# Reordering the FFN's first product pair, its passage from up to down, and its last squares in a fused two-layer block

## The chip, the cores and the metric

One core of one Trainium2 chip runs the whole program once per launch. The metric is device microseconds of that core, the median of several runs. The engines work side by side, each with its own in-order instruction stream, and meet at semaphores: PE (TensorE), ACT (ScalarE), DVE (VectorE), POOL (GpSimd) and SP (SyncE, which here only issues DMAs). ACT can issue DMAs too, on a queue of its own.

## The reference

A sequence of 1024 tokens with 1024 features goes through two layers. The change lies in the feed-forward part (FFN) of the first layer and in what stands next to it:

```python
    u2 = _rmsnorm(h, ln2_g[i])
    a, bb = jnp.split(u2 @ w_gate_upffn[i], 2, axis=-1)      # 1024 -> 2 x 2816
    h = h + (jax.nn.silu(a) * bb) @ w_down[i]                # 2816 -> 1024
    u3 = _rmsnorm(h, ln3_g[i])
    gate = jax.nn.sigmoid(u3 @ w_ple_gate[i])
    h = h + gate * (p[i] @ w_ple_proj[i])                    # p: 256 -> 1024
```

Before it stand gated linear attention and a convolution with their projection; after it a second layer with window attention.

## The kernel before

All tensors are held feature-major, 128 partitions by 1024 tokens per tile. Each fp32 operand is split in a rounded high part (`_hi`) and a rest (`_lo`), and each product is three matmuls (hi·hi, hi·lo, lo·hi). The FFN's matrix products are done by a seven-product scheme (Strassen and Winograd's), so for each weight slot `w` there are seven combinations `r = 0..6` of quarters of the weights and of the operand.

**The projection of p** (`gemm4`, L751) is the last thing ahead of the FFN: eight output tiles of 1024 tokens, written to the PSUM halves G[0] and G[1] in turn, and copied out by ACT (`projected_p`, L1417) to `pj_out`, from where SP sends them to memory.

**The up stage** has 22 slots, w = 0..21 (`UP` = 22), even ones for `a` in G, odd ones for `bb` in U. `product(w, r)` (L939) does 12 matmuls of 512 columns: it waits for `ring_lo` of (w, r), for w < 2 also for `X_lo[r]`, and for the PSUM banks to be read. The first and the last two slots (0 and 1; 20 and 21) go in the order of the list `FIRST`: (0,0) (0,1) (1,0) (1,1) (0,2) (0,3) (1,2) (1,3) (0,4) (0,5) (0,6) (1,4) (1,5) (1,6). ACT rounds weights (`weights_hi`, L1425 to L1433, to `ring_hi`) and operands (`operand_hi`, L1435, to `X_hi`); DVE makes the rests (`weights_lo` L2090, `operand_lo` L2083), the normalised input (`normed_x` L2066, four instructions each) and the operand's differences (`turn_x` L2072). POOL makes the weights' sums S (`sums_of`, L606). ACT and DVE read the products from PSUM (`take` L1448, `quarter` L2095), and ACT's `silu` (L1462) and DVE's `gated_quarter` (L2110) end a pair of slots, which is a group.

**The hidden values.** A group's result `cb` is turned into seven pieces by four DVE differences (`turn_h`, L2118). Each piece is rounded by ACT (`hidden_hi`, L1467), its rest is made by DVE (`hidden_lo`, L2129), both in `hst[q % 2]`, two buffers used in turn, and SP sends it to `hid_spill` in memory (`hidden_out`, L468). With 11 groups there are 77 pieces, q = 0..76; the last group's are 70 to 76. ACT may write a buffer only when the DMA of two pieces before has landed (semaphores `hs_out`).

**The down stage** reads the pieces back, two groups (a chunk) at a time, as 14 DMAs of 512 KB (`chunk_in`, L476) into Dc[0] (0 to 56 KB of each partition, where X_hi[0..3] and X_lo[0..3] lie) or Dc[1] (56 to 112 KB). `down_product` (L967) does 12 matmuls a slot and r, in two halves m; products 4, 5 and 6 wait until DVE has added the first products of the same slot to `h` (`down_add`, L2184 to L2196). `h` itself was sent to memory before the FFN and comes back in two DMAs of 2 MB (`h_in`), since `cb` and `hst` lie in its place. Each engine's order is written out by hand. SP's order in the passage from up to down: weights of slot 22, pieces 63 and 64, chunk 0 rows 0 to 3, pieces 65 and 66, chunk 0 rows 4 to 6, pieces 67 to 69, weights 23, first half of h, pieces 70 and 71, and so on (`chunks_in`, L500 to L531).

**The end of the FFN.** In the last slot (`LAST` = 32) DVE puts four squares (`add_square`) among its adds; POOL makes the rests of A3's tiles 0 to 3 and then both parts of the first weight slot of the next product (`split(1, S_PLE)`, L642). Behind that PE starts `gemm(1, S_PLE, ...)`, and then `gemm(0, S_PLE + 1, ...)`, ahead of whose tile 1 it sums the squares (`quarter_sums`) and ahead of whose tile 4 it spreads the inverse root (`spread`, L925 to L931).

## Time and profile before

| | us |
|---|---|
| median of three runs | 1735.76 (1732.69 to 1735.9) |
| the profiled execution, by itself | 1733.72 |
| its span, first to last instruction | 1731.9 |
| PE busy | 1648.4 (95%) |
| DVE / POOL / ACT busy | 1167.1 / 703.1 / 623.9 |
| mean granted TensorE clock | 0.986 of full |

Spans are read from the first instruction's start; us from the span's start are called times below. PE's own share of 95% leaves some 83 us in which it is idle, and the mean clock of 0.986 tells of stretches in which it ran at half speed.

### The profile page before, as it was taken

The page shows a single profiled execution, that of the slowest core. Times are in us where ns is not written, and L with a number is a line of the kernel's source. Part 1 is how long each engine was busy: PE and PEld are TensorE (multiplying, and loading weights), DVE is VectorE, ACT ScalarE, POOL GpSimd, SP SyncE. Part 2 cuts the span into 40 slices and gives each one's busy share as a digit, 9 for nine tenths or more (in the row PEclk, how much of TensorE's full clock was granted, in tenths as well). Part 3 has the DMA queues.
Part 4 walks back from the last instruction along what each step waited for, and adds up shares of the span by engine and source line. Part 5 has one row for each costly group of instructions (what it writes and reads, how often), then busy time and mean ns, then how long its engine had stood idle before and what let it go on. Part 6 is the DMA issues. An engine that isn't in the chain of part 4 may idle for free.

```text
span 1731.9 us, 21560 instructions
## 1 busy us (share of the span) xinstructions
PE 1648.4 (95%) x7810; PEld 1358.0 (78%) x7810; DVE 1167.1 (67%) x1697; ACT 623.9 (36%) x976; POOL 703.1 (41%) x381
## 2 busy tenths in 40 slices
PE   9999999999979999999997899999879999999996
PEld 6888787878868888888885788877658888889775
DVE  7232898953497777776757566878856983685457
ACT  5131333321345444444433122254451111277214
POOL 2534111144423332332226587652255554452451
PEclk9999999999999999999999999999999999999998
DMA  5411110141613434334377966041101111100012
GB/s 189 82 49 39 35 37 25 37 158 49 219 61 134 158 135 164 151 147 169 151 285 283 374 267 269 27 158 49 37 12 49 48 49 49 61 26 1 25 37 97
DMA packets 52421, 190.24 MB, mean 110 GB/s; under 512 B 5681, under 2 KB 7618, under 8 KB 51562
## 3 DMA queue, kind: packets, MB, share of 16 engines
q1 hardware_dynamic: 49378, 178.95, 28.5%
q10 hardware_dynamic: 2952, 10.10, 2.3%
q8 instruction: 55, 0.90, 0.2%
q14 instruction: 36, 0.29, 0.1%
HBM read 133.97 MB, written 55.05 MB: 109 GB/s over the span
## 4 chain that ended last, share of the span: by engine, by line
PE 56%; DVE 8%; DMA 3%; issue 3%; ACT 2%; POOL 1%; POOLq 0%; DVEq 0%; ACTq 0%
PE G L730 15%; PE U L962 11%; PE G L962 10%; PE U L1000 5%; PE G L1000 5%; PE G L1036 2%; PE U L1210 2%; DMA hid_spill<-hst 2%; PE G L1197 1%; PE G L1116 1%; PE U L1079 1%; DVE h L2196 1%; DVE B_lo L1821 1%; DMA h<-h_spill 0%; DVE hst L2132 0%
## 5 line engine op out<-in xcount | busy, mean ns | idle before, releaser
L581 POOL TENSOR_SCALAR w_hi<-raw 128x1024 fp32r<-128x1024 f32 x51 | 152.8, 2997 | 298.4 <-PE G L730 220.6
L730 PE MATMUL G<-B_hi,w_hi 128*128 128x512 f32 x512 | 161.3, 396 | 5.1 <-DVE h L2054 2.8
L730 PE MATMUL G<-B_lo,w_hi 128*128 128x512 f32 x512 | 158.7, 391 | 0.0
L730 PE MATMUL G<-B_hi,w_lo 128*128 128x512 f32 x512 | 158.5, 391 | 0.0
L730 PE MATMUL G<-A_hi,w_hi 128*128 128x512 f32 x448 | 144.6, 404 | 2.9 <-DVE h L2196 2.8
L730 PE MATMUL G<-A_lo,w_hi 128*128 128x512 f32 x448 | 138.9, 391 | 0.0
L730 PE MATMUL G<-A_hi,w_lo 128*128 128x512 f32 x448 | 138.6, 391 | 0.0
L583 POOL TENSOR_TENSOR w_lo<-raw,w_hi 128x1024 fp32r<-128x1024 f32 x51 | 134.6, 2639 | 4.3
L619 POOL TENSOR_TENSOR S<-fraw 128x512 f32<-128x512 f32 x33 | 45.9, 1390 | 217.4 <-DVE ring_lo L2093 200.1
L962 PE MATMUL U<-X_hi,ring_hi 128*128 128x512 f32 x308 | 121.4, 394 | 9.6 <-DVE ring_lo L2093 9.6
L1433 ACT ACTIVATE ring_hi<-S 128x512 fp32r<-128x512 f32 x132 | 82.1, 628 | 115.2 <-PE U L1000 76.4
L962 PE MATMUL G<-X_hi,ring_hi 128*128 128x512 f32 x308 | 120.1, 390 | 2.5 <-ACT pj_out L1420 1.2
L962 PE MATMUL U<-X_lo,ring_hi 128*128 128x512 f32 x308 | 120.8, 392 | 0.0
L962 PE MATMUL U<-X_hi,ring_lo 128*128 128x512 f32 x308 | 120.8, 392 | 0.0
L962 PE MATMUL G<-X_lo,ring_hi 128*128 128x512 f32 x308 | 119.9, 389 | 0.0
L962 PE MATMUL G<-X_hi,ring_lo 128*128 128x512 f32 x308 | 119.8, 389 | 0.0
L730 PEld LDWEIGHTS G<-B_hi,w_hi 128*128 128x128 f32 x512 | 96.3, 190 | 27.5 <-DVE h L2054 3.2
L730 PEld LDWEIGHTS G<-B_lo,w_hi 128*128 128x128 f32 x512 | 96.9, 189 | 20.5
L730 PEld LDWEIGHTS G<-B_hi,w_lo 128*128 128x128 f32 x512 | 96.7, 189 | 20.3
L1433 ACT ACTIVATE ring_hi<-fraw 128x512 fp32r<-128x512 f32 x99 | 61.8, 627 | 114.6 <-PE U L1000 61.0
L1000 PE MATMUL G<-Dc,ring_hi 128*128 128x512 f32 x280 | 88.5, 398 | 14.3 <-DVE h L2196 14.3
L730 PEld LDWEIGHTS G<-A_hi,w_lo 128*128 128x128 f32 x448 | 84.4, 188 | 18.2
(377 smaller groups left out, 3837.2 us busy)
## 6 DMA issues: line engine op xcount, KB each, us to landing
hid_spill<-hst SPq DMA_DIRECT2D x77, 512.0 KB, 2.6
raw<-in_weights SPq DMA_DIRECT2D x72, 512.0 KB, 3.6
Dc<-hid_spill SPq DMA_DIRECT2D x70, 512.0 KB, 7.8
fraw<-in_weights SPq DMA_DIRECT2D x66, 512.0 KB, 4.5
h<-in_x_t SPq DMA_DIRECT2D x8, 512.0 KB, 7.7
h<-in_x_t ACTq DMA_DIRECT2D x1, 4096.0 KB, 15.1
h_spill<-h SPq DMA_DIRECT2D x8, 512.0 KB, 6.7
pj_spill<-pj_out SPq DMA_DIRECT2D x8, 512.0 KB, 2.6
```

What stands on the lines that cost most here:

```text
L581: pool.tensor_scalar(hi, raw[:, u, :], 1.0, None, ALU.mult).then_inc(w_hi_done, 1)
L583: pool.tensor_tensor(lo, raw[:, u, :], f(hi), ALU.subtract).then_inc(w_split, 1)
L619: pool.tensor_tensor(s1, a21, a22, ALU.add).then_inc(s_sum, 1)
L730: mm = pe.matmul(G[g][:, b * HT:(b + 1) * HT], w, x[:, k, b * HT:(b + 1) * HT], start=s0, stop=s1)
L962: mm = pe.matmul(banks[x][BANK_OF[r]], a, b[r][:, k, :], start=(r < 4 and k == 0 and n == 0), stop=(k == 3 and n == 2), skip_group_check=( ...
L1000: mm = pe.matmul(banks[m][BANK_OF[r]], a, b, start=(r < 4 and n == pairs[0] and e == 0), stop=(n == pairs[-1] and e == 2), skip_group_chec ...
L1036: mm = pe.matmul(G[g][:, hs(n)], a, x[:, kk, hs(n)], start=(kk == 0 and e == 0), stop=(kk == KT - 1 and e == 2))
L1079: mm = pe.matmul(U[:, b, g * P:(g + 1) * P], first, sm[:, n, row, :], start=True, stop=True)
L1116: mm = pe.matmul(G[u][:, hs(n)], w, x[:, k, hs(n)], start=(k == 0 and not low and e == 0), stop=(k == KT - 1 and low == 1))
L1197: mm = pe.transpose(G[0][:, hd % 2 * HT + kb * P:hd % 2 * HT + (kb + 1) * P], scores_of(n, par, hd)[:, kb * P:(kb + 1) * P], ident[:, :])
L1210: mm = pe.matmul(U[:, 2 + par, c0:c0 + HD], pT[:, hd % 2, kb, :], vv, start=(kb == 0), stop=(kb == nkb - 1))
L1433: act.activation(ring(ring_hi, w, r), combo(w, r), ACT.Copy).then_inc(f_hi[w % 2], 1)
```

## The change

It has three parts. In the first pair, the last tile of the projection of p is computed and copied out by halves of 512 tokens (new semaphore `p_half`, new function `last_projected`), and ACT's and DVE's orders are changed. In the passage, the last five pieces get buffers of their own (`hst_last`, seven with the two of `hst`), the 14 DMAs of chunk 0 move from SP's queue to ACT's (`first_chunk_in`), SP's order is changed, and ACT rounds the last seven pieces in one run. At the end, the high part of weight slot S_PLE moves from POOL to ACT, and two of the four squares move behind the adds.

```diff
+        hst_last = [at(f"hst_last{j}", kb, [P, 2, HT], F32R) for j, kb in enumerate((96, 100, 104, 108, 196))]
...
+        def piece_of_pair(q):
+            own = q - NR * (GROUPS - 1) - 2
+            return hst[:, q % 2, :, :] if own < 0 else hst_last[own][:, :, :]
...
             def hidden_out(q):
+                landed_in = hs_out[q % 2] if q < NR * (GROUPS - 1) + 2 else hs_last
                 sp.wait_ge(hl_done, q + 1)
...
             last = NR * (GROUPS - 2)
-            hidden_out(last), hidden_out(last + 1)
-            chunks_in(0, UP - 1, 0, 1, 2, 3)
-            hidden_out(last + 2), hidden_out(last + 3)
-            chunks_in(0, UP - 1, 4, 5, 6)
-            for j in range(4, NR):
+            for j in range(NR):
                 hidden_out(last + j)
             raw_in(UP + 1)
...
             h_in(0)
             last += NR
-            hidden_out(last), hidden_out(last + 1)
+            for j in range(NR):
+                hidden_out(last + j)
+            for u in range(2):
+                sp.wait_ge(hs_out[u], 16 * (last // 2 + 1))
+            h_in(1)
             raw_in(UP + 2)
-            hidden_out(last + 2), hidden_out(last + 3)
-            for j in range(4, NR):
-                chunks_in(1, UP - 1, j - 4)
-                hidden_out(last + j)
-            landed(GROUPS)
-            h_in(1)
-            chunks_in(1, UP - 1, 3, 4, 5, 6)
+            chunks_in(1, UP - 1, 0, 1, 2, 3, 4)
+            sp.wait_ge(hs_last, 16 * len(hst_last))
+            chunks_in(1, UP - 1, 5, 6)
             raw_in(UP + 3)
...
-            pool.wait_ge(f_used[0], used(LAST, 2))
-            split(1, S_PLE, bufs[1], wait=False)
+            weights_low(S_PLE, bufs[1])
...
                 if w == 0 and r == 0:
+                    pe.wait_ge(p_half, 2)
+                if w == 0 and r == 1:
                     pe.wait_ge(acc_free[0], (C_PLE + 1) // 2)
...
+                elif r == 3:
+                    act.wait_ge(w_split, S_PROJ + 2)
...
+                if q >= NR * (GROUPS - 1) + 2:
+                    act.wait_ge(f_used[1], used(UP - 1, NR - 1))
+                elif q >= 2:
...
+            def last_projected():
+                g = (C_PROJ + KT - 1) % 2
+                act.wait_ge(p_half, 1)
+                act.activation(pj_out[:, (KT - 1) % 2, (KT - 1) // 2, 0:HT], G[g][:, 0:HT], ACT.Copy).then_inc(p_half, 1)
+                act.wait_ge(acc_done, C_PROJ + KT)
+                act.activation(pj_out[:, (KT - 1) % 2, (KT - 1) // 2, HT:T], G[g][:, HT:T], ACT.Copy).then_inc(acc_free[g], 1)
...
+            def first_chunk_in(r):
+                for n in range(2):
+                    act.dma_start(f(Dc[0][:, r, n, :, :].rearrange("p a n -> p (a n)")), hid_spill[n, :, r, :]).then_inc(ch_in[0][r], 16)
...
                     hidden_hi(NR * (GROUPS - 2) + hi_at[k])
+                if x and r < 4:
+                    first_chunk_in(2 * r)
+                    if r < 3:
+                        first_chunk_in(2 * r + 1)
             last = NR * (GROUPS - 1)
-            hidden_hi(last), hidden_hi(last + 1)
+            for j in range(NR):
+                hidden_hi(last + j)
             for w in range(UP, LAST):
                 for r in range(NR):
                     weights_hi(w + 1, r)
-                    if w == UP and r < 5:
-                        hidden_hi(last + 2 + r)
...
+            act.wait_ge(f_used[0], used(LAST, 2))
+            slot_hi(S_PLE, w_hi[:, 1, :], wait=False)
             act.wait_ge(f_used[0], used(LAST, 5))
...
             turn_h(last, 0), hidden_lo(NR * last), turn_h(last, 1), hidden_lo(NR * last + 1), turn_h(last, 2)
+            hidden_lo(NR * last + 2), hidden_lo(NR * last + 3), turn_h(last, 3)
             dve.wait_ge(h_back[0], 16)
             for r in range(NR):
                 down_add(r, 0, UP, 0, 0)
-                if r < 5:
-                    hidden_lo(NR * last + 2 + r)
-                if r == 2:
-                    turn_h(last, 3)
+                if r < 3:
+                    hidden_lo(NR * last + 4 + r)
...
-                    if w == LAST and r < 4:
+                    if w == LAST and r < 2:
                         add_square(r % 2, 2 * KT + r, 2 * KT + r)
```

`gemm4` gets the argument `halves`, with which its last tile does the six matmuls of tokens 0 to 511 and then the six of tokens 512 to 1023. The two squares taken out stand among the four `A_lo` instructions behind the adds.

The first pair on DVE, from the eight instructions of the normalised input on (`X_lo_101` to `_104` are X_lo[0] to X_lo[3], `ring_lo_126`, `_127`, `_128` are r = 0, 1, 2, `fraw_110` is slot 0's weights and `fraw_111` slot 1's). Before:

```order
L2070 SCALAR_TENSOR_TENSOR h<-h,vecs,U 128x512 x8
L2088 TENSOR_TENSOR X_lo_101<-h,X_hi_94 128x2048
L2093 TENSOR_TENSOR ring_lo_126<-fraw_110,ring_hi_119 128x512
L2093 TENSOR_TENSOR ring_lo_127<-fraw_110,ring_hi_120 128x512
L2088 TENSOR_TENSOR X_lo_102<-h,X_hi_95 128x2048
L2070 SCALAR_TENSOR_TENSOR h<-h,vecs,U 128x512 x4
L2081 TENSOR_TENSOR T1x<-h 128x2048
L2093 TENSOR_TENSOR ring_lo_128<-S_133,ring_hi_121 128x512
L2070 SCALAR_TENSOR_TENSOR h<-h,vecs,U 128x512 x4
L2093 TENSOR_TENSOR ring_lo_126<-fraw_111,ring_hi_119 128x512
```

Now (`ring_lo_131`, `_132`, `_133` are the same three buffers):

```order
L2106 SCALAR_TENSOR_TENSOR h<-h,vecs,U 128x512 x8
L2124 TENSOR_TENSOR X_lo_101<-h,X_hi_94 128x2048
L2124 TENSOR_TENSOR X_lo_102<-h,X_hi_95 128x2048
L2129 TENSOR_TENSOR ring_lo_131<-fraw_110,ring_hi_124 128x512
L2129 TENSOR_TENSOR ring_lo_132<-fraw_110,ring_hi_125 128x512
L2106 SCALAR_TENSOR_TENSOR h<-h,vecs,U 128x512 x4
L2117 TENSOR_TENSOR T1x<-h 128x2048
L2129 TENSOR_TENSOR ring_lo_133<-S_138,ring_hi_126 128x512
L2129 TENSOR_TENSOR ring_lo_131<-fraw_111,ring_hi_124 128x512
L2106 SCALAR_TENSOR_TENSOR h<-h,vecs,U 128x512 x4
```

X_lo[1] has moved ahead of the first two weight rests, and slot 1's first rest ahead of the last four instructions of the normalised input. On ACT, `X_hi[0]` and `X_hi[1]` have moved ahead of the first three `ring_hi`.

The passage on DVE, from the first difference of the last group on. Before:

```order
L2127 TENSOR_TENSOR T1h<-cb 128x512
L2132 TENSOR_TENSOR hst<-cb,hst 128x512
L2127 TENSOR_TENSOR cb<-cb 128x512
L2132 TENSOR_TENSOR hst<-cb,hst 128x512
L2127 TENSOR_TENSOR T2h<-cb,T1h 128x512
L2196 TENSOR_TENSOR h<-h,G 128x512
L2196 TENSOR_TENSOR h<-h,U 128x512
L2132 TENSOR_TENSOR hst<-T1h,hst 128x512
```

Now:

```order
L2163 TENSOR_TENSOR T1h<-cb 128x512
L2169 TENSOR_TENSOR hst<-cb,hst 128x512
L2163 TENSOR_TENSOR cb<-cb 128x512
L2169 TENSOR_TENSOR hst<-cb,hst 128x512
L2163 TENSOR_TENSOR T2h<-cb,T1h 128x512
L2169 TENSOR_TENSOR hst_last_119<-T1h,hst_last_119 128x512
L2169 TENSOR_TENSOR hst_last_120<-cb,hst_last_120 128x512
L2163 TENSOR_TENSOR cb<-cb,T2h 128x512
L2233 TENSOR_TENSOR h<-h,G 128x512
L2233 TENSOR_TENSOR h<-h,U 128x512
```

Eight instead of five instructions stand ahead of the first add to `h`, and behind it three rests instead of five and a difference.

## Rows read from the trace of the kernel before

**Rows 1.** Waits of PE, whole span: us in total, times, longest.
```profile
PE G L1000 <- DVE h L2196: 14.3, 4, 4.8
PE U L962 <- DVE ring_lo L2093: 9.6, 4, 4.3
```
**Rows 2.** Timeline of PE, first pair: start, us, what, idle before and its releaser.
```profile
481.40 0.47 PE L962 MATMUL G<-X_hi,ring_hi 128*128 128x512 f32 x1 [1.21 <-ACT pj_out L1420]
...
489.48 0.50 PE L962 MATMUL U<-X_hi,ring_hi 128*128 128x512 f32 x1 [2.36 <-DVE ring_lo L2093]
...
506.15 0.79 PE L962 MATMUL U<-X_hi,ring_hi 128*128 128x512 f32 x1 [4.31 <-DVE ring_lo L2093]
```
**Rows 3.** Chain that ended last, first pair and after: start, us, what.
```profile
506.15 8.31 PE U L962 x24
...
550.46 19.04 PE U L962 x84
```
**Rows 4.** Timeline of ACT, first pair.
```profile
470.27 1.14 ACT L1433 ACTIVATE ring_hi<-fraw 128x512 fp32r<-128x512 f32 x2
...
472.99 1.91 ACT L1445 ACTIVATE X_hi<-h 128x2048 fp32r<-128x2048 f32 x1
```
**Rows 5.** Timeline of DVE, first pair.
```profile
474.93 2.29 DVE L2088 TENSOR_TENSOR X_lo<-h,X_hi 128x2048 fp32r<-128x2048 f32 x1 [2.92 <-ACT X_hi L1445]
...
480.55 2.71 DVE L2070 SCALAR_TENSOR_TENSOR h<-h,vecs,U 128x512 f32<-128x512 f32 x4
```
**Rows 6.** Timeline of PE in the passage, rows that follow an idle time.
```profile
912.69 0.50 PE L962 MATMUL U<-X_hi,ring_hi 128*128 128x512 f32 x1 [2.62 <-DVE ring_lo L2093]
...
930.04 0.70 PE L1000 MATMUL G<-Dc,ring_hi 128*128 128x512 f32 x2 [3.46 <-DVE h L2196]
...
941.96 1.19 PE L1000 MATMUL G<-Dc,ring_hi 128*128 128x512 f32 x2 [4.75 <-DVE h L2196]
...
962.20 1.11 PE L1000 MATMUL G<-Dc,ring_hi 128*128 128x512 f32 x2 [4.83 <-DVE h L2196]
```
**Rows 7.** The chain that ended last, in the passage.
```profile
890.25 9.58 DMA hid_spill<-hst
...
953.28 8.06 DMA h<-h_spill
```
**Rows 8.** Stretches: us, then PE, PEld, DVE, ACT, POOL busy, granted clock, DMA share, GB/s.
```profile
962.00:967.00 5.00, 4.80 (x14) 3.87 (x15) 5.00 (x10) 0.19 (x1) 0.00 (x0) 0.66 1.03 419
1144.00:1150.00 6.00, 3.16 (x8) 2.46 (x8) 5.28 (x8) 4.11 (x5) 4.86 (x3) 0.72 0.80 306
```
**Rows 9.** Timeline of DVE in the passage.
```profile
920.87 1.68 DVE L2127 TENSOR_TENSOR T1h<-cb 128x512 f32<-128x512 f32 x1
...
929.22 0.67 DVE L2196 TENSOR_TENSOR h<-h,G 128x512 f32<-128x512 f32 x1
```
**Rows 10.** Timeline of SP's queue in the passage.
```profile
883.18 4.60 SPq L478 DMA_DIRECT2D Dc<-hid_spill  x8
...
959.38 19.32 SPq L478 DMA_DIRECT2D Dc<-hid_spill  x14
```
**Rows 11.** Timeline of PE at the end of the FFN.
```profile
1146.97 1.22 PE L730 MATMUL G<-A_hi,w_hi 128*128 128x512 f32 x2 [2.84 <-DVE h L2196]
...
1165.64 1.89 PE L931 MATMUL U<-R,ident 128*128 128x256 f32 x8
```
**Rows 12.** Timeline of ACT at the end of the FFN.
```profile
1159.88 1.06 ACT L1555 ACTIVATE w_hi<-raw 128x1024 fp32r<-128x1024 f32 x1 [4.04 <-PE G L730]
```
**Rows 13.** Timeline of DVE at the end of the FFN.
```profile
1162.76 1.75 DVE L2064 RECIPROCAL R<-R 128x256 f32<-128x256 f32 x1 [4.41 <-ACT R L1415]
```
**Rows 14.** Timeline of POOL at the end of the FFN.
```profile
1140.42 3.74 POOL L581 TENSOR_SCALAR w_hi<-raw 128x1024 fp32r<-128x1024 f32 x1
1144.25 2.36 POOL L583 TENSOR_TENSOR w_lo<-raw,w_hi 128x1024 fp32r<-128x1024 f32 x1
```
**Rows 15.** The `raw` DMA issued at 1146.78 (tile raw, 1146 to 1148).
```profile
DMA to landing us min/median/max: 12.1/12.1/12.1
```

More of the change, by code:

```diff
@@ L468, in hidden_out @@
             def hidden_out(q):
+                landed_in = hs_out[q % 2] if q < NR * (GROUPS - 1) + 2 else hs_last
                 sp.wait_ge(hl_done, q + 1)
-                sp.dma_start(hid_spill[q // NR, :, q % NR, :], f(hst[:, q % 2, :, :].rearrange("p a n -> p (a n)"))).then_inc(hs_out[q % 2], 16)
-            def landed(pairs):
-                for u in range(2):
-                    sp.wait_ge(hs_out[u], 16 * ((NR * pairs + 1 - u) // 2))
+                sp.dma_start(hid_spill[q // NR, :, q % NR, :], f(piece_of_pair(q).rearrange("p a n -> p (a n)"))).then_inc(landed_in, 16)
             def chunk_in(c, r):
@@ L749, in gemm, with gemm4 @@
                           last=acc_done if k == KT - 1 else after.get(k))
[L751 removed]
+            def gemm4(u, s, a, g, hi, lo, k0, between=None, halves=False):
                 pe.wait_ge(w_split, s + 1)
@@ L758, in gemm4 @@
                     pe.wait_ge(acc_free[gg], a + (g + b) // 2)
+                    if halves and b == 3:
+                        for n in range(2):
+                            for k in range(2):
+                                wh, wl = (w[:, u, (2 * b + k) * P:(2 * b + k + 1) * P] for w in (w_hi, w_lo))
+                                for e, (w, x) in enumerate(((wh, hi), (wh, lo), (wl, hi))):
+                                    mm = pe.matmul(G[gg][:, n * HT:(n + 1) * HT], w, x[:, k0 + k, n * HT:(n + 1) * HT],
+                                                   start=(k == 0 and e == 0), stop=(k == 1 and e == 2))
+                            mm.then_inc(acc_done if n else p_half, 1)
+                        continue
                     for k in range(2):
@@ L1500, in _ @@
                 weights_hi(2, r)
+            def first_chunk_in(r):
+                for n in range(2):
+                    act.dma_start(f(Dc[0][:, r, n, :, :].rearrange("p a n -> p (a n)")), hid_spill[n, :, r, :]).then_inc(ch_in[0][r], 16)
             hi_at = {0: 0, 1: 1, 3: 2, 4: 3, 6: 4, 7: 5, 9: 6}
@@ L2131, in hidden_lo @@
                 dve.wait_ge(hh_done, q + 1)
-                dve.tensor_tensor(hst[:, q % 2, 1, :], h_src[q % NR], f(hst[:, q % 2, 0, :]), ALU.subtract).then_inc(hl_done, 1)
+                hi, lo = (piece_of_pair(q)[:, e, :] for e in range(2))
+                dve.tensor_tensor(lo, h_src[q % NR], f(hi), ALU.subtract).then_inc(hl_done, 1)
             inverse_q(2)
@@ L2222, in _ @@
                 low(A3_hi, A3_lo, k, k, h[:, k, :], 2 * KT + k, col("ln3", k))
-                if k > 4:
-                    add_square(k % 2 ^ 1, 2 * KT + k - 1, 2 * KT + k - 1)
-            add_square(1, 3 * KT - 1, 3 * KT - 1)
+                add_square(k % 2, 2 * KT + k - 2, 2 * KT + k - 2)
+            for k in range(KT - 2, KT):
+                add_square(k % 2, 2 * KT + k, 2 * KT + k)
             def gate_in(k):
```

39 lines of the change are left out of this document (21 added, 18 removed).

## The prediction

> **What bounds the kernel now.** I read the waits of PE first, since PE is busy for 95% of the span (the table above). Two lines of that view matter: the adds of the down stage hold PE up for 14.3 us in 4 places, the rests of the weights in the up stage for 9.6 us in 4 [rows 1]. The timeline of PE places them. In the first pair PE stops before products (0,0), (1,0) and (1,2) for 1.21, 2.36 and 4.31 us [rows 2], and between the last two once more, for 0.9 before (0,3). In the passage it stops for 2.62, 3.46, 4.75 and 4.83 us, the last three for the adds [rows 6]; the 1.2 us that remain of the 14.3 are a stop between them. At the end of the FFN it stops once more, for 2.84 us [rows 11]. These are all its waits of over 0.4 us from the first pair to there, so each of the three places is local: what is saved in one moves the end, unless a later wait takes it back.
>
> A stop has two further prices. The first is a refill: the first matmul behind a stop takes 0.47 to 0.79 us [rows 2], one in the flow 0.39, and the last one ahead of it drains; I put 0.3 us on each. The second is the clock. A slot of 84 matmuls takes 19.04 us [rows 3], 0.227 us each; behind the stop of 4.31 us, 24 matmuls took 8.31 us [rows 3] instead of 5.44, so 2.9 us went to the lower level of 1.2 GHz. Behind the stop of 4.83 us the granted clock was 0.66 over 5 us, behind that of 2.84 us it was 0.72 over 6 us [rows 8]: 1.7 us lost each. No such stretch follows the stops of 2.36 and 3.46 us. So here a stop of over 4 us has lost the clock each time, and one of about 3 us may.
>
> **The first pair.** DVE is what PE waits for, and DVE itself waited 2.92 us for X_hi[0] [rows 5], because ACT did three `ring_hi` from 470.27 on and began X_hi[0] at 472.99 [rows 4]. In the new order X_hi[0] begins at 470.3 and ends at 472.2. From there I go forward on DVE: 2.2 us from start to start for a 2048-wide instruction, 2.6 for four of the normalised input [rows 5], 0.6 for a 512-wide one, which lasts 0.67 [rows 9]. X_lo[0] ends at 474.4. X_hi[1] is there at 474.9, X_lo[1] ends at 477.1, two rests at 478.3, four inputs at 481.0, T1x at 483.2, two more rests at 484.5. The last of these is slot 1's first. PE now starts at 480.0, since half of the last tile of the projection is copied out beside the other half's matmuls, and comes to product (1,0) at 485.5: the stop of 2.36 us is gone. Four inputs, a rest, X_lo[2], a difference and a rest end at 492.8; X_hi[3] holds DVE until 494.2, and X_lo[3] ends at 496.5. PE is at (0,3) by 493.6 and waits 3.0 us. T2x and the rest of (1,2) end at 499.3, when PE gets there, so the stop of 4.31 us is gone. At (0,5) I get another 1.3 us, behind two reads of PSUM. Idle falls from 9.1 us (the four stops and one of 0.3 in slot 2) to 4.3, and three refills go: 5.7 us. Of the clock's 2.9 us, 1.7 may be lost again behind the stop of 3.0 us; I count half of that and keep 2.0. **First pair: 7.7 us**, bounds 6.9 and 8.6.
>
> **The passage.** Two waits come from DMAs. The pieces wait for their two buffers: one write of 512 KB took 9.58 us [rows 7], queued on SP's queue behind eight reads of the chunk. And the last write must land before the second half of h is read, whose 8.06 us end in the stop of 4.83 us [rows 7]. Both go, with chunk 0 on ACT's queue and five more buffers. The second read of h now stands behind the issue of piece 76, at about 934, and lands 8 us later, at 942; it is first needed before slot 23's fifth product, at 912.2 + 7 + 19.0 + 10.9 = 949.
>
> What is late next is DVE. Slot 21's last product starts at 912.69 [rows 6]; without the stops of 2.6 and 0.3 us ahead of it and a refill it ends at 912.2, and four products of slot 22 need no add, so PE arrives at the fifth at 923.1. DVE ends the last group's gating at about 918; before, ACT's late pieces had put that off to 920.87. Then eight instructions stand ahead of the first add, not five. The five took 929.22 - 920.87 = 8.35 us [rows 9], 1.67 each, while POOL's sums and rests ran; alone such an instruction takes 0.6. With six at 1.7 and two at 0.6, as POOL runs out of work, the first add starts at about 929, and PE goes on at 929.5, against 930.04 before [rows 6]. So the stop at this place grows from 3.46 to 5.8 us (gain 0.5 over all), 0.9 us follow at the sixth product, and the clock is lost once, 1.6. Gone are 1.2, 4.75 and 4.83 us (10.8) and the low clock behind the last two (3.3). **Passage: 0.5 + 10.8 + 3.3 - 0.9 - 1.6 = 12.1 us.** The least I take as 5, a second stop like that of 4.83 us with its clock staying; the most is 19.5, all eight instructions at 0.6: then the first add comes at 923, and 5.8 + 1.6 more are won.
>
> The 14 issues on ACT are new work on a path that others wait for. Eight on SP took 4.60 us, 0.57 each [rows 10], so they take 8 us within the pair's 38. They hold back ACT's reads of PSUM by up to 2.3 us. I count nothing for them: the products that wait for these, from (1,4) on, have about 3 us of room.
>
> The Trainium skill ("DMA: Bandwidth & Descriptors", "Rules for kernel authors") speaks against this part: spreading DMAs over SP and ACT brings no bandwidth, since all of them run on the same engines. By it the writes would land as late as before, and the sum would be some 3 us less. The same page ("Queues, rings and completion order") lets each DMA engine take turns between queues, so that a write on one needn't stand behind the reads on the other. No row here shows that.
>
> **The end.** The adds now follow PE by 0.7 us, without the two squares. POOL reaches the first weights at 1140.42, with only the rest of 2.36 us to make [rows 14] instead of both parts, so they are ready by 1142.8, and PE goes on at 1144 without the stop of 2.84 us and the 1.7 us of clock: 4.5 us. But a wait behind it stays where it was. The second weights' DMA stands behind 4 MB of `pj`, issued when PE ends the FFN, and landed at 1146.78 + 12.1 = 1158.9 [rows 15]. ACT rounds them ahead of the root, and began that at 1159.88 [rows 12]; the reciprocal behind the root ended at 1162.76 + 1.75 = 1164.5 [rows 13], 4.6 us later. From 1158.9 on it ends at 1163.5, and the spread ran at 1165.64 [rows 11]. **End: 2.2 us**, with a new stop of some 2.3 ahead of the spread. Bounds: 0.5, if that stop costs the clock, and 4.5, if the DMA lands sooner.
>
> The sum is 7.7 + 12.1 + 2.2 = 22.0 us. Against the profiled execution's own 1733.72 that gives 1711.7. Two of the three runs shown lie 2 us above that execution and one lies 1 us below; I take 1712 for the median.
>
> **The rivals.**
> - *DVE isn't slowed.* POOL's seven rests and four sums need 14 us. If they fall ahead of DVE's eight instructions, the first add is in time: 1712 - 7.4 = 1704.6. Against it: the five before were all slowed [rows 9]. 0.16.
> - *The writes land as late as before*, because bandwidth, and not their place in SP's queue, made the 9.58 us. The stop of 2.62 us stays with its refill: 1715. For it: the DMA share was 1.03 in a stretch like this one [rows 8]. This is what the skill's first rule would do here. 0.12.
> - *ACT is held by its queue.* Later on 14 such issues took 19.32 us, 1.38 each [rows 10]. That adds 0.8 x 14 = 11 us on ACT, of which some 8 reach PE: 1720. Against it: the eight issued first, as here, went at 0.57. 0.10.
> - *The same on the other side.* Were all 14 issues held for 2.5 us each, nearly twice that average, ACT would be stopped for 35 us instead of 8. If all of it reaches PE, 1712 + 27 = 1739, slower than before. It decides from 2.1 us an issue on: (2.1 - 0.57) x 14 = 21.5. 0.03.
> - *The passage gains nothing*, since its DMAs are the bound: 16.3 MB stand between 914 and the end of chunk 1 (twice 2.1 of h, 3.7 of pieces, 1.05 of weights, 7.3), 39 us at the 419 GB/s of [rows 8]. Then 1724. Against it: at that rate chunk 1's first row is there at 938, and it is needed at 957. 0.04.
>
> **How the numbers follow.** Forecast 0.55, rivals 0.16, 0.12, 0.10, 0.03, 0.04. The range of 1702 to 1722 takes in the first three rivals and most of the bounds, and leaves out the other two and the corners. A measurement of this kernel tells about 0.2% (3.5 us) from no change. Faster 0.95, within 0.02, slower 0.03.
>
> **What would show it.** Right: product (1,0) without a stop and one of about 3 us at (0,3); ACT's pieces no longer waiting for `hid_spill`; one stop of 5 to 6 us in slot 22 and none from there to 1120; one of about 2 us ahead of the spread. Wrong: ACT's reads of PSUM in the last pair late by over 3 us, which is its issues; a second long stop, in slot 23, which is h; or the first add before 925, which is DVE's share with POOL.

## Result, and the profile after

| | us |
|---|---|
| median after, 5 runs | 1713.04 (1710.17 to 1714.56) |
| median before, 5 runs beside it | 1735.34 (1732.69 to 1735.9) |
| ratio | 0.9872, 95% interval 0.9858 to 0.9887 |
| profiled execution after, by itself | 1711.62, its span 1709.8 |
| mean granted TensorE clock | 0.988 of full (0.986 before) |

The medians differ by 22.3 us, the two profiled executions by 22.1. The forecast was 22.0. (Measured a second time, below, the whole change gave 18.9.) The three parts did not come out as it had them, though. To see that, I read the start of PE's rows at five marks, in every profile: the first matmul of the last projection, slot 3's first, slot 20's, slot 30's, and the spread. The stretches between the marks hold one part of the change each, and the others act as a control: slots 3 to 20 took 323.7 us in every kernel here.

| PE, us from mark to mark | first pair | passage | slot 30 to spread |
|---|---|---|---|
| before | 94.61 | 212.33 | 79.33 |
| after | 90.39 | 199.50 | 76.14 |
| gain | 4.2 | 12.8 | 3.2 |
| forecast | 7.7 | 12.1 | 2.2 |

That makes 20.2. The other 2.0 us lie ahead of the change: the projection began at 453.66 instead of 455.69, with the same instructions before it. In the fourteen profiles of this study it began between 453.2 and 457.0, so 2 us is within what single executions differ by. So I don't count it as a gain, and that the sum came out to a tenth is luck.

The waits of PE after, from the page's view of waits (us in total, times, longest), between 440 and 1200 us. The first two answer to [rows 1]:

```profile
PE G L1011 <- DVE h L2233: 5.8, 1, 5.8
PE G L973 <- DVE X_lo L2124: 2.9, 1, 2.9
...
PE U L973 <- DVE ring_lo L2129: 1.0, 2, 0.5
PE G L973 <- DVE ring_lo L2129: 0.9, 1, 0.9
PE U L932 <- DVE acc L1851: 0.7, 1, 0.7
PE U L940 <- DVE R L2100: 0.4, 1, 0.4
```

One wait for the adds is left of four, and 1.9 us for the rests of weights instead of 9.6. The timeline of PE, its rows behind an idle time, answers to [rows 2, 6, 11]:

```profile
494.60 0.77 PE L973 MATMUL G<-X_hi,ring_hi 128*128 128x512 f32 x1 [2.87 <-DVE X_lo L2124]
495.16 0.63 PE L973 MATMUL G<-X_lo,ring_hi 128*128 128x512 f32 x1
...
508.63 0.51 PE L973 MATMUL G<-X_hi,ring_hi 128*128 128x512 f32 x1 [0.95 <-DVE ring_lo L2129]
...
923.78 1.19 PE L1011 MATMUL G<-Dc,ring_hi 128*128 128x512 f32 x2 [5.85 <-DVE h L2233]
...
1137.97 0.64 PE L932 MATMUL U<-acc,ones 128*32 128x256 f32 x8 [0.67 <-DVE acc L1851]
...
1143.37 1.99 PE L940 MATMUL U<-R,ident 128*128 128x256 f32 x8 [0.45 <-DVE R L2100]
```

Between the stops at 923.78 and 1137.97 PE is idle for 0.1 us in all: both late stops of the passage and the one at the end of the FFN [rows 6, 11] are gone. Behind 494.60 seven matmuls start 0.43 us apart or more, not 0.227, before the pitch is back at 0.23: that is the lower level of the clock. The stretches show it in the granted clock (the third number from the end of a row), behind the stop of 2.87 and behind that of 5.85:

```profile
495.00:500.00 5.00, 5.00 (x17) 3.97 (x17) 4.71 (x4) 0.92 (x2) 0.00 (x0) 0.73 0.00 0
...
923.00:928.00 5.00, 4.22 (x10) 3.40 (x11) 5.00 (x10) 2.71 (x5) 3.70 (x3) 0.52 0.84 332
```

The timeline of DVE at the passage answers to [rows 9]: six instructions at 1.7, two at 0.68, then the first add.

```profile
911.72 1.67 DVE L2163 TENSOR_TENSOR T1h<-cb 128x512 f32<-128x512 f32 x1
...
920.08 1.75 DVE L2169 TENSOR_TENSOR hst_last<-T1h,hst_last 128x512 fp32r<-128x512 f32 x1
921.76 0.68 DVE L2169 TENSOR_TENSOR hst_last<-cb,hst_last 128x512 fp32r<-128x512 f32 x1
922.36 0.68 DVE L2163 TENSOR_TENSOR cb<-cb,T2h 128x512 f32<-128x512 f32 x1
922.96 0.68 DVE L2233 TENSOR_TENSOR h<-h,G 128x512 f32<-128x512 f32 x1
```

### The profile page after: what moved, and what is told of

Read it like the earlier page. It is cut to its first block, busy times and chain, and to the rows that moved or that the text cites. A ratio compares the mean times of both kernels' runs of the same rounds, so it can differ in the third digit from the quotient of the medians.

```text
span 1709.8 us, 21563 instructions
## 1 busy us (share of the span) xinstructions
PE 1643.1 (96%) x7810; PEld 1355.6 (79%) x7810; DVE 1166.5 (68%) x1697; ACT 625.4 (37%) x978; POOL 699.1 (41%) x380
## 4 chain that ended last, share of the span: by engine, by line
PE 73%; DVE 14%; DMA 5%; issue 3%; ACT 3%; POOL 1%; ACTq 0%; DVEq 0%; POOLq 0%; SPq 0%
PE G L730 28%; PE U L973 10%; PE G L973 10%; PE U L1011 6%; PE G L1011 6%; DMA bias_scratch<-fvec 3%; PE G L1047 2%; PE U L1221 2%; DMA h<-in_x_t 1%; PE U L876 1%; PE G L1208 1%; DVE B_lo L1857 1%; DVE qt L1930 1%; DVE X_lo L2124 1%; PE U L1090 1%
## 5 line engine op out<-in xcount | busy, mean ns | idle before, releaser
L583 POOL TENSOR_SCALAR w_hi<-raw 128x1024 fp32r<-128x1024 f32 x50 | 148.7, 2974 | 294.7 <-PE G L730 217.8
L730 PEld LDWEIGHTS G<-A_lo,w_hi 128*128 128x128 f32 x448 | 84.4, 188 | 18.0
```

The costliest lines, as they stand in the source:

```text
L583: pool.tensor_scalar(hi, raw[:, u, :], 1.0, None, ALU.mult).then_inc(w_hi_done, 1)
L730: mm = pe.matmul(G[g][:, b * HT:(b + 1) * HT], w, x[:, k, b * HT:(b + 1) * HT], start=s0, stop=s1)
```

## Each part alone, and the whole again

Each edit puts the code of the other two parts back as it was before. The fourth run has no edit. The diffs are long; these are lines from them, against the changed kernel. Of the passage put back:

```diff
-            own = q - NR * (GROUPS - 1) - 2
+            own = -1
...
-                if x and r < 4:
-                    first_chunk_in(2 * r)
```

Of the first pair put back, and of the end:

```diff
-            gemm4(0, S_PROJ + 1, C_PROJ // 2 + 2, 1, p_hi, p_lo, 0, halves=True)
+            gemm4(0, S_PROJ + 1, C_PROJ // 2 + 2, 1, p_hi, p_lo, 0)
...
-            operand_lo(0), operand_lo(1), weights_lo(0, 0), weights_lo(0, 1)
+            operand_lo(0), weights_lo(0, 0), weights_lo(0, 1), operand_lo(1)
```
```diff
+            pool.wait_ge(f_used[0], used(LAST, 2))
+            split(1, S_PLE, bufs[1], wait=False)
...
-            weights_low(S_PLE, bufs[1])
...
-            act.wait_ge(f_used[0], used(LAST, 2))
-            slot_hi(S_PLE, w_hi[:, 1, :], wait=False)
```

> Only the first pair's part of the change, the passage and the end as before. Theory (three independent places, each worth what lies between two marks in the two traces): from the start of the projection of p to the start of slot 3 it saves 4.2 us (94.8 before, 90.5 after), so 1731 us for 1735.3. By the prediction's own sum 7.7 us, 1727.6. Rival (the first pair's gain depends on what follows): under 2 us or over 7.

> Only the passage's part (seven buffers, chunk 0 on ACT's queue, SP's and DVE's orders). Theory of independent places: 12.8 us between the starts of slot 20 and of the single group's slot 30, one stop of 5 to 6 us in slot 22, 1722.5 us. Rival: without the earlier first pair SP or POOL stand differently to PE and the stop is another one: under 10 us.

> Only the end's part (high part of slot S_PLE on ACT, two squares moved). Theory of independent places: 3.2 us from the start of slot 30 to the spread, since the DMA behind pj holds ACT; about 1732. By the rival that the fixed wait isn't there: 4.5 us, 1731. If the squares were a burden behind the adds: under 1 us.

> The changed kernel itself, beside its parts on one chip. Theory: its gain is the sum of the three parts' within 2 us, some 20 to 22 us. Rival (parts overlap or help one another): off by over 4 us.

Measured, with 1733.72 as the median of 19 runs of before beside them:

| | median | ratio, 95% | first pair | passage | to spread |
|---|---|---|---|---|---|
| first pair alone | 1729.29 | 0.9967 to 0.9995 | 86.77 | 213.19 | 79.55 |
| passage alone | 1720.26 | 0.9906 to 0.9957 | 94.72 | 199.77 | 77.92 |
| end alone | 1728.72 | 0.9958 to 0.9983 | 93.83 | 213.23 | 76.14 |
| whole again | 1714.82 | 0.9855 to 0.9918 | 91.48 | 198.80 | 76.09 |

Each part moves its own stretch and no other beyond 1.4 us, so the three places are local, as forecast. (The 1.4 is the end of "passage alone", 77.92 for 79.33: the same stop of 2.84 us stands there, but with the clock kept behind it, 24 matmuls in 5.57 us and not in 6.99.) In its profile the passage gives 12.6 alone and the end 3.2. The profile of the first pair alone gives 7.8, just what was forecast, but those of the whole kernel 4.2 and 3.1, with the same instructions.

One profile is one execution, though, and by the medians the picture is less clean: 4.4 us for the first pair (0.9 to 5.7 by its interval, which leaves out the 7.7 forecast), 13.5 and 5.0 for the others, together 22.9, and 18.9 for the whole again (14 to 25 by its interval). The theory of the fourth run, a sum within 2 us, is missed by both readings, 4.0 us by the medians and 3.7 by the marks (7.8 + 12.6 + 3.2 against 3.1 + 13.5 + 3.2). By the marks it is the first pair that makes the difference. The rows of PE of the first pair alone show the same stop and no slow matmul behind it:

```profile
497.94 0.47 PE L980 MATMUL G<-X_hi,ring_hi 128*128 128x512 f32 x1 [2.86 <-DVE X_lo L2124]
498.25 0.40 PE L980 MATMUL G<-X_lo,ring_hi 128*128 128x512 f32 x1
498.48 0.39 PE L980 MATMUL G<-X_hi,ring_lo 128*128 128x512 f32 x1
```

So the question left open was the first pair: is it the clock, and why does it cost 3.6 us where some 1.7 were counted?

## The passage: what bounds it now

**Chunk 0 on SP's queue again.**

```diff
-                if x and r < 4:
-                    first_chunk_in(2 * r)
-                    if r < 3:
-                        first_chunk_in(2 * r + 1)
...
-            for j in range(NR):
-                hidden_out(last + j)
+            hidden_out(last), hidden_out(last + 1)
+            chunks_in(0, UP - 1, 0, 1, 2, 3)
+            hidden_out(last + 2), hidden_out(last + 3)
+            chunks_in(0, UP - 1, 4, 5, 6)
+            for j in range(4, NR):
+                hidden_out(last + j)
```

> Chunk 0 is read by SP again, between its writes of the pieces; all else as changed. Theory (the writes landed late since they stood behind the reads on SP's own queue): the write of 884.3 takes 9.6 us again instead of 6.8, ACT waits for it 2.6 us longer and PE stops for 2 to 3 us in the last pair; the 14 issues on ACT, 8.9 us, go, and give nothing back: passage 202 to 203 us instead of 199.5, time 1716. Rival A (bandwidth makes the time of a write): 6.8 us here too and no stop: 1713 or, if ACT's issues held someone up, 1711. Rival B (the old stop was the buffers' alone, and two writes ahead are enough): no stop, 1713.

Measured: 1710.45 (ratio 0.9855 to 0.9895), passage 199.92. Its chain and its PE:

```profile
882.08 9.43 DMA hid_spill<-hst
```
```profile
904.36 0.71 PE L977 MATMUL U<-X_hi,ring_hi 128*128 128x512 f32 x1 [2.61 <-DVE ring_lo L2129]
...
922.90 0.70 PE L1015 MATMUL G<-Dc,ring_hi 128*128 128x512 f32 x2 [3.05 <-DVE h L2233]
```

The mechanism is as the theory had it: the write takes 9.43 us again, against 6.82 in the changed kernel, and the stop of 2.6 in the last pair is back. But it gives no time, which the theory had wrong. The next stop shrinks by as much, from 5.85 to 3.05, since DVE's first add comes at its own time (922.08) whenever PE gets there. So the move of the chunk is worth 0.1 to 1.1 us (199.92 against 198.80 to 199.79 in the six profiles whose passage is otherwise the same) as long as DVE is late behind it. That this kernel's median lies below the 1713.04 of the changed one is no gain of the passage; its profile kept the clock in the first pair (86.79).

Piece by piece over all fourteen profiles, with the chunk's reads on ACT's queue (ten) against both on SP's (four): the write of piece 65 took 6.6 to 8.1 us against 9.4 to 9.6, that of piece 66 7.4 to 7.9 against 8.2 to 8.6, but that of piece 64, which now runs beside the reads and not ahead of them, 5.5 to 6.1 against 3.0 to 3.1. The median of the 14 reads was 7.8 to 8.3 against 8.6 to 8.7. The longest stop in the last pair was at most 1.4 with two queues and 2.6 each time with one. The Trainium skill ("DMA: Bandwidth & Descriptors", "Rules for kernel authors") says that spreading DMAs brings no bandwidth; the runs bear it out in part: piece 65 gains about 2 us by its place in the queue, which is not all that stood ahead of it, and piece 64 loses nearly 3.

**POOL's sums late, and DVE's old order.** Two ways to bring the first add forward. In the first, POOL makes slot 23's sums only when DVE has its fourth rest:

```diff
             for w in range(UP, LAST + 1):
+                if w == UP + 1:
+                    pool.wait_ge(hl_done, NR * GROUPS - 3)
                 sums_of(w)
```

> POOL's four sums of slot 23 wait until DVE has made its fourth rest of the last group. Theory (DVE's eight instructions ahead of the first add take 1.7 us each because POOL works beside them, as T1h at 911.72 did): two of them fall beside POOL's last rests, six take 0.6, so the first add starts at about 918.7, ahead of PE's arrival at 923. The stop of 5.84 us in slot 22 and the clock behind it go, 7.4 us: 1705.6 against 1713.0, the passage 192 us instead of 199.5. Rival A (they are slow for another cause, their operands or PSUM): still 1.7 each, the stop stays, 1713. Rival B (the late sums hold up ACT's rounding of slot 23's third weights and PE behind it): the stop moves to slot 23, gain under 3 us.

In the second, DVE has its order of before (five instructions, then adds and rests in turn):

```diff
-            hidden_lo(NR * last + 2), hidden_lo(NR * last + 3), turn_h(last, 3)
             dve.wait_ge(h_back[0], 16)
             for r in range(NR):
                 down_add(r, 0, UP, 0, 0)
-                if r < 3:
-                    hidden_lo(NR * last + 4 + r)
+                if r < 5:
+                    hidden_lo(NR * last + 2 + r)
+                if r == 2:
+                    turn_h(last, 3)
```

> DVE's old order at the passage: five instructions ahead of the first add of down instead of eight, the rest between the adds. Theory (the stop in slot 22 is the count of slow instructions ahead of the first add): five at 1.7 from 911.7 put it at 920.2, ahead of PE's arrival at 923, so the stop of 5.84 us and the clock behind it go, as much as 7.4 us: 1705.6. Rival (the instructions between the adds are what PE waits for next): the first adds come in time but the third and fourth, behind slow rests at 1.7, are late, and a stop of 2 to 4 us stands at the sixth to eighth product: 1708 to 1711.

Late sums measured 1707.59 (0.9834 to 0.9876), passage 196.05; its timeline of DVE:

```profile
911.88 1.67 DVE L2165 TENSOR_TENSOR T1h<-cb 128x512 f32<-128x512 f32 x1
913.48 1.78 DVE L2171 TENSOR_TENSOR hst<-cb,hst 128x512 fp32r<-128x512 f32 x1
915.18 0.68 DVE L2165 TENSOR_TENSOR cb<-cb 128x512 f32<-128x512 f32 x1
...
918.19 0.68 DVE L2165 TENSOR_TENSOR cb<-cb,T2h 128x512 f32<-128x512 f32 x1
919.92 0.69 DVE L2235 TENSOR_TENSOR h<-h,G 128x512 f32<-128x512 f32 x1 [1.05 <-DMA h<-h_spill]
```

Two instructions at 1.7 beside POOL's last rests, six at 0.68 with POOL at rest until the last of them: POOL is what slows DVE here. This was one change with nothing else moved, so I call it shown. The passage gained 3.4 us, not 7.4, for two reasons. I had PE arrive at 923, the forecast's figure, which counts by the times of the kernel before; in the changed one, where slot 20 begins 6.25 us earlier, it is there at 917.9. And DVE, now ready at 918.8, waits 1.05 us for the first half of h, whose read is issued when the gating ends (911.87) and lands 8.03 later. That sets the floor of this place: the first add ends at 920.6, and PE stops for 2.68 us, with the clock lost behind it.

The old order measured 1714.54 (0.9872 to 0.9914) and a passage of 203.82, slower than theory and rival alike. The first add came at 919.24, held by the same read of h, and the stop at the fifth product was 3.25, again with the clock lost. But the pieces' last rest came later, SP's queue with it, and a wait that was in no forecast appeared in slot 24, for POOL's rest of weights. The DMA that brings them took 16.44 us, no longer than in the changed kernel (17.16), but it was issued 83.9 us behind the start of slot 20 instead of 78.7:

```profile
972.26 1.22 PE L1011 MATMUL G<-Dc,ring_hi 128*128 128x512 f32 x2 [2.28 <-POOL ring_lo L637]
```

So fewer instructions ahead of the first add do bring it forward, and the rest between the adds then sets SP's queue back. The rival was right that it comes back, wrong on where.

## The first pair: the clock, and what follows it

**Filling the stop.** PE makes matmuls of no use in the time that it would wait for X_lo[3]:

```diff
                 pe.wait_ge(f_lo[x], turn(w, r))
+                if w == 0 and r == 3:
+                    for k in range(11):
+                        pe.matmul(banks[x][BANK_OF[r]], ring_hi[r][:, 0:P], X_hi[2][:, k % 4, :], start=True, stop=True)
```

> PE makes 11 matmuls of no use (they write the bank that product (0,3) then begins anew) ahead of its wait for X_lo[3], 2.5 of the 2.87 us of that stop. Theory (the chance part of the first pair is the clock behind this stop, which was lost in three of the six profiles of this order of instructions, 90.4 to 91.5 us from the projection's start to slot 3, and kept in the three others, 86.8): 86.8 us, the granted clock 1.0 in all stretches behind it, and the runs lie in the lower half of the changed kernel's, 1711 in the median. Rival (the clock is lost for what comes ahead of the stop or by the stretch of time, whatever PE does in it): 90 us or a coin's toss, 1713.

Measured: 1709.88 (0.9837 to 0.9878), first pair 86.80. PE's timeline, and a stretch behind it with the granted clock at 1.00:

```profile
491.44 2.65 PE L955 MATMUL G<-X_hi,ring_hi 128*128 128x512 f32 x11
494.38 0.50 PE L976 MATMUL G<-X_hi,ring_hi 128*128 128x512 f32 x1 [0.28 <-DVE X_lo L2127]
```
```profile
495.00:500.00 5.00, 5.00 (x23) 3.83 (x22) 5.00 (x5) 2.54 (x3) 0.00 (x0) 1.00 0.00 0
```

Without the fill this stop of 2.86 to 2.87 us was profiled six times: three times the lower clock followed (90.39, 91.48 and 90.48 to slot 3), three times not (86.77, 86.80, 86.79). With the fill it was profiled twice, and the clock stayed both times (86.80, 86.77). Two of two against three of six doesn't prove it. PE's work was the only thing changed, and the median is lower by 3.2 us; but against its own runs of before the gain is only 2.6 us larger (0.9857 for 0.9872), the intervals overlap, and the kernel with chunk 0 on SP's queue, which has no fill, measured 1710.45. So that the fill keeps the clock fits all that was seen and isn't shown. What it doesn't do is shorten the stretch: with the clock kept, 86.8 us stand with the fill and without it.

**Why 3.6 and not 1.7.** From the start of the twelve matmuls behind the stop to the start of the next product it took 4.28 us in the changed kernel, and 2.80 to 2.84 in the three kernels with the same stop that kept the clock: 1.5 us. (In the whole measured again the low level lasted longer, 5.26 us: 2.5.) The chain that ended last shows the twelve with the end of the last one:

```profile
494.60 4.46 PE G L973 x12
```

The other 2.1 are mostly further stops. With the clock lost, PE makes product (0,3) later, ACT rounds the weights of (1,3), which wait for it, later, X_hi[4] comes behind them, and DVE waits for both. In that gap POOL gets in with a sum. DVE and POOL of the changed kernel:

```profile
499.75 1.30 DVE L2129 TENSOR_TENSOR ring_lo<-S,ring_hi 128x512 fp32r<-128x512 f32 x2 [0.29 <-ACT ring_hi L1446]
501.55 3.02 DVE L2124 TENSOR_TENSOR X_lo<-T2x,X_hi 128x2048 fp32r<-128x2048 f32 x1 [0.51 <-ACT X_hi L1458]
```
```profile
501.13 1.30 POOL L626 TENSOR_TENSOR S<-S,fraw 128x512 f32<-128x512 f32 x1 [8.97 <-DVE ring_lo L2129]
```

And of the kernel with DVE's old order at the passage, whose first pair is the same and kept the clock:

```profile
501.80 2.28 DVE L2124 TENSOR_TENSOR X_lo<-T2x,X_hi 128x2048 fp32r<-128x2048 f32 x1
```
```profile
501.96 5.47 POOL L626 TENSOR_TENSOR S<-S,fraw 128x512 f32<-128x512 f32 x1 [8.60 <-DVE ring_lo L2129]
```

Whichever engine is under way when the other comes keeps its speed: DVE 3.02 and POOL 1.30 in the one, DVE 2.28 and POOL 5.47 in the other. The same happens again at X_lo[6] (3.38 at 509.10 against 2.28 at 508.61). So PE stops for 0.95, 0.90, 0.50 and 0.34 us instead of for 0.98 and 0.35: 1.4 us more, and two more refills. That this is the order of cause is read from the traces and wasn't tested by itself, but all eight profiles of this order agree: in the three that lost the clock X_lo[4] took 3.01 to 3.02 and X_lo[6] 3.38, in the five that kept it neither was slowed.

**Removing the stop instead.** DVE makes its second difference ahead of X_lo[2], so that ACT's X_hi[3] runs beside X_lo[2]:

```diff
-            weights_lo(1, 1), operand_lo(2), turn_x(1)
+            weights_lo(1, 1), turn_x(1), operand_lo(2)
```

> In the first pair DVE makes the second difference of x ahead of X_lo[2], so that ACT's X_hi[3] runs beside X_lo[2] and DVE's wait of 1.38 us for it goes. Theory (the clock is at stake only behind the stop of 2.87 us at product (0,3)): a stop of 1.3 us appears at (0,2), the one at (0,3) falls to under 0.5, 1.4 us less idle, and no product runs at the low clock: from the projection's start to slot 3 about 85.5 us in every profile, against 90.4 and 91.5 of the two with the clock lost and 86.8 of the one without. Time 1709. Rival (the clock falls at random, whatever the stop): a stretch at the low clock here too, 88 to 90 us, time 1712.

Measured: 1712.60 (0.9867 to 0.9907), first pair 90.74. The stop at (0,3) is gone and one of 1.27 stands at (0,2), as expected; but at (1,3) (the next expectation has it as (1,2)) a new one of 1.81 us came, with the clock at 0.66 behind it. Its cause is POOL, whose sum S3, which before had fallen into DVE's wait of 1.38 us, now stood beside DVE's 2048-wide instructions. ACT waited for it, DVE for ACT, and PE for DVE:

```profile
490.67 8.27 POOL L623 TENSOR_TENSOR S<-fraw 128x512 f32<-128x512 f32 x1 [7.17 <-DVE ring_lo L2129]
```
```profile
499.06 0.63 ACT L1446 ACTIVATE ring_hi<-S 128x512 fp32r<-128x512 f32 x1 [5.29 <-POOL S L623]
```
```profile
500.47 0.65 PE L973 MATMUL U<-X_hi,ring_hi 128*128 128x512 f32 x1 [1.81 <-DVE ring_lo L2129]
```

The theory that only the stop of 2.87 puts the clock at stake is refuted by this row: one of 1.81 did too. The next run moves the sum:

```diff
-            weights_lo(0, 2), weights_lo(1, 0)
+            weights_lo(0, 2), weights_lo(1, 0), weights_lo(0, 3)
...
-            weights_lo(1, 1), operand_lo(2), turn_x(1)
-            weights_lo(0, 3), operand_lo(3), turn_x(2)
+            weights_lo(1, 1), turn_x(1), operand_lo(2)
+            operand_lo(3), turn_x(2)
```

> As the run that made the second difference of x first, and the rest of (0,3) besides ahead of the last four normalised inputs, so that POOL's sum S3, which took 8.27 us beside DVE's 2048-wide instructions, runs beside instructions that read PSUM. Theory (POOL starves beside 2048-wide instructions of DVE and not beside those from PSUM): the sum takes 1.3 to 1.7 us, the stop of 1.81 us at (1,2) goes, and with stops of about 1.3 at (0,2) and 0.9 at (0,5) and (0,6) the stretch to slot 3 is 85.5 us; time 1709. Rival A (it starves wherever DVE is busy): the sum takes over 5 us again, 90 us to slot 3. Rival B (DVE is the bound all along, so what is gained at (0,3) comes back at (0,5)): 86.8 us, 1711.

Measured: 1711.44 (0.9853 to 0.9895), first pair 89.26. The sum took what the theory said, beside instructions that read PSUM, with a DVE that was not slowed:

```profile
483.92 1.31 POOL L623 TENSOR_TENSOR S<-fraw 128x512 f32<-128x512 f32 x1 [0.63 <-DVE ring_lo L2129]
```
```profile
483.76 2.71 DVE L2106 SCALAR_TENSOR_TENSOR h<-h,vecs,U 128x512 f32<-128x512 f32 x4
```

But the stretch is no shorter than the 86.8 of the changed kernel with its clock kept; it is 2.5 us longer. PE stopped for 1.24 at (1,1), 1.44 at (0,2), 1.80 at (0,5) and 0.93 at (0,6), though the clock stayed at 1.00 from 490 to 520. That is rival B, and worse: what DVE does earlier for one product it does later for another. It isn't DVE's own work alone, though. Three of its instructions were stretched beside POOL in this run, the moved rest at 482.06 to 1.78 us (0.68 alone) and X_lo[5] and X_lo[6] to 3.39 and 3.37 (2.28 alone), 3.3 us together, and none of the three was so in the kernels that kept 86.8. Whether this order would be as fast without these meetings is not tested.

The next run has the same order, and there the clock was lost behind the same stop at (0,5). The stretches 507 to 512 us, first of this run, then of the next, have the granted clock at 1.00 and at 0.66:

```profile
507.00:512.00 5.00, 3.80 (x16) 2.86 (x17) 4.87 (x5) 1.83 (x4) 1.67 (x1) 1.00 0.58 204
```
```profile
507.00:512.00 5.00, 4.24 (x12) 3.34 (x13) 4.87 (x5) 1.70 (x4) 1.66 (x1) 0.66 0.51 185
```

The first pair took 89.26 us with the clock kept and 89.32 with it lost: PE spent at the lower level the time in which it otherwise waited for DVE at (0,6). So the price of a lost clock goes from nothing to 3.6 us and more, by what stands behind it.

## Put together, and the end of the FFN

```diff
-            slot_hi(S_PLE + 2, w_hi[:, 1, :])
             root_q(3, "eps")
+            slot_hi(S_PLE + 2, w_hi[:, 1, :])
```

This edit, the late sums and the first pair's last order were run together:

> The late sums of slot 23, the first pair's order of the run before this one, and at the end ACT makes the root ahead of rounding the second weights, whose DMA lands late. If the parts add: first pair 85.5, passage 196.0, and from slot 30 to the spread 75.7 instead of 76.1 us, since the stop of 0.45 us ahead of the spread was ACT held by the DMA: 1702.5. Rival: the first pair gains nothing, 1707, or the weights rounded later hold PE up behind the spread, a stop of over 1 us there that eats the 0.4.

Measured: 1710.93 (0.9852 to 0.9898); 89.32, 197.48 and 75.53. The forecast of 1702.5 is missed by 8.4 us, and even the rival's 1707 was too low: the first pair gained nothing, as the rival said, and the passage stopped for 3.84 us at the fifth product, since DVE was ready at 917.4 but the first half of h landed 8.40 us behind its issue. Then the same with the fill in place of that order, and a second fill:

```diff
+                    if d == 0 and r == 3 and m == 0:
+                        for k in range(10):
+                            pe.matmul(banks[m][BANK_OF[r]], ring(ring_hi, w, r)[:, 0, m, :], Dc[0][:, r, 0, 0, :], start=True, stop=True)
                     for n in pairs:
```

> The parts that helped, put together: the matmuls of no use at (0,3), slot 23's sums late, the root ahead of the second weights' rounding, and as a second test of filling 10 more matmuls of no use ahead of slot 22's fourth product, in time that PE would otherwise spend waiting at the fifth. Theory (a stop that PE fills costs its idle time and no clock): first pair 86.8 us; passage 194.7, 1.3 us less than the 196.05 of the run with late sums alone, the granted clock 1.0 behind slot 22's fifth product; slot 30 to the spread 75.6. Sum: 1713.0 - 3.6 - 3.4 - 1.3 - 0.5 = 1704.2. Rival (the fourth product's own add is what PE needs next, so 2.3 us more ahead of it return as a stop): passage 196 to 197, 1706.

Measured: 1707.70 (0.9829 to 0.9874), for 1704.2 forecast; 86.77, 198.76 and 75.52.

The end is as expected in both. In the changed kernel ACT waited for the DMA ahead of the root, and without that wait PE's stop ahead of the spread is gone. ACT after, and ACT in the last kernel:

```profile
1138.68 1.06 ACT L1589 ACTIVATE w_hi<-raw 128x1024 fp32r<-128x1024 f32 x1 [2.26 <-DMA raw<-in_weights]
1139.76 1.28 ACT L1426 ACT_TABLE_LOAD   x1
1141.05 0.47 ACT L1426 ACTIVATE R<-U,vecs 128x256 f32<-128x256 f32 x1
```
```profile
1136.45 0.48 ACT L1434 ACTIVATE R<-U,vecs 128x256 f32<-128x256 f32 x1 [0.96 <-PE U L934]
1136.82 1.05 ACT L1597 ACTIVATE w_hi<-raw 128x1024 fp32r<-128x1024 f32 x1
```

The second fill brought nothing. The stop at the fifth product fell from 2.68 to 0.58, with the clock at 1.00 behind it, and one of 2.85 came at the sixth, with the clock at 0.66 behind it. The sixth waits for the third add, and two rests of DVE ahead of that add met one of POOL's late sums and the first rest behind them with POOL already under way (by 0.06 and 0.01 us), which they had not done in the run with late sums alone (0.68 at 921.12, POOL's sum at 921.20):

```profile
919.08 1.79 DVE L2177 TENSOR_TENSOR hst_last<-T2h,hst_last 128x512 fp32r<-128x512 f32 x1
...
922.00 1.80 DVE L2177 TENSOR_TENSOR hst_last<-cb,hst_last 128x512 fp32r<-128x512 f32 x1
```

The two slow rests cost 2.2 us; without them I estimate a stop of 0.6 at the sixth product. So this run doesn't decide what the fill itself is worth.

Neither combination is faster than the late sums alone, 1707.59, which needs one wait. Its median is 5.5 us below the changed kernel's, but 2.9 by the ratios to their own runs of before (0.9855 and 0.9872), whose intervals (0.9834 to 0.9876 and 0.9858 to 0.9887) overlap; it can't be told from the last kernel's 1707.70. The passage varies by 2.7 us between the three kernels with late sums, with the landing of h and with who holds DVE's and POOL's way.

## Why the prediction was right, and where its terms were not

**First pair, 7.7 forecast, 4.2 measured, 7.8 alone.** DVE's order came out nearly to the tenth. With the start 2.0 us earlier, X_lo[0] was forecast to end at 472.4 and ended at 472.45, X_lo[3] at 494.5 and ended at 494.45; the stop at (0,3) was 2.87 for 3.0, (1,0) and (1,2) had none, and with the clock kept PE was idle for 4.1 to 4.2 us in the pair, for 4.3. The term that failed is the clock: "1.7 may be lost again behind the stop of 3.0 us; I count half of that". Such a stop loses it or not, as a whole: 86.8 or 90.4 to 91.5. When lost, it took 3.6 to 4.7 us here and not 1.7, since PE's lateness goes round through ACT and DVE to its own next operands. The lower bound of 6.9 was thus too high by 2.7 to 3.8.

**Passage, 12.1 forecast, 12.8 measured, 12.6 alone.** The stop in slot 22 was 5.85 for 5.8, with eight instructions as counted; the late stops are gone; the second half of h was issued at 928.9 and landed at 937.3, which, with slot 20 beginning 6.25 us earlier here, is 1 to 1.5 us behind the 934 and 942 of the forecast, and PE never waited for it. The stop of 0.9 at the sixth product, forecast from the adds, did not come, and neither did the gain of 0.5 at the fifth: PE went on at 923.78, which is 930.0 by the times of the kernel before. What the forecast had not said is that the parts of this place aren't additive: the chunk's move, which takes away the stop of 2.6 us, gives next to nothing while DVE's first add sets the time.

**End, 2.2 forecast, 3.2 measured, 3.2 alone.** The chain is as forecast: DMA, rounding, root, and 4.63 us from ACT's rounding to the reciprocal's end for 4.6. The mis-sized step is the DMA's landing, which I left at 1158.9. It is issued behind POOL's rest of the first weights (1144.25 + 2.36 = 1146.61, the DMA at 1146.78 [rows 14, 15]), and the change makes that rest early. After, the issue came 1.3 us behind the end of the FFN, not 2.7, so it landed 1.1 us earlier against it. The new stops are 0.67 and 0.45, not 2.3. Some 1.4 of the 3.2 us is the clock behind the old stop of 2.84 us, which the kernel before lost and "passage alone", with the same stop, kept; so this gain too has a part of chance.

**The rivals.** "DVE isn't slowed" was not so: 1.7 us each, as counted; made so by the late sums it would not have given 7.4 us either, for the read of h is the next bound. "The writes land as late as before" was so in part: 6.82 for 9.58 in the changed kernel, but up to 8.9 in others with the same queues, whose stops of 1.4 the next wait took up. "ACT is held by its queue": the 14 issues took 8.9 us where 8 were counted, and the reads of PSUM were not late by a time that PE shows. The whole was right, 1712.0 for 1713.04, because +0.7 at the passage and +1.0 at the end stood against -3.5 in the first pair, and 2.0 of the profile's gain lie ahead of the change. The mechanisms of the passage and the end came out as told; the total did by luck, and the whole again, at 18.9 us, did not repeat it. Two of the prediction's figures are off by a tenth: (2.1 - 0.57) x 14 is 21.4, and 1165.64 - 1163.5 is 2.1.

## To carry to other kernels

Where two waits end in one place, work out what comes second before you sum: a gain ahead of a wait that keeps its own time is a gain of nothing. A short stop of PE that may lose the clock is no half term but two cases, each with what the lower clock then makes late. If PE has something harmless to do in the stop, such as matmuls into a bank that is begun anew, it may keep the clock; two profiles of two fit that here, and no more. And when a step moves, look for every DMA whose issue waits for it.

## Of the hardware, not expected

- Whether the lower clock follows a stop is not decided by its length between 1.8 and 3.5 us. In the fourteen profiles, between 440 and 1200 us, it was lost behind 1.81 (twice), 2.28, 2.60 to 2.62 (three times), 2.68, 2.83, 2.84, 2.85 and 3.25; kept behind 1.80, 2.36 to 2.37 (four times), 2.62, 2.84, 3.04, 3.05, 3.09 and 3.46; 2.86 to 2.87 went both ways, three times each. The stop in the last pair and the one at the end of the FFN also went both ways with the same code around them. Behind each stop of 3.84 us and more it was lost.
- DVE and POOL working on SBUF at once do not share evenly. One POOL sum of 128x512 took 1.3 us alone, 8.27 beside DVE's 2048-wide instructions, and 5.47 another time, with DVE at full speed; met the other way, DVE's 2.28 became 3.02 and 3.38, and its 0.68 became 1.7 to 1.8 while POOL kept to 1.3 to 1.7. Beside DVE instructions with an operand in PSUM the sum took 1.31; it took 1.61 where it began 0.2 us behind the start of a DVE rest in SBUF.
